# Hybrid attention block: the first branch's value products as [query, 64] from unnormalised probabilities

## The chip, the cores and the metric

The kernel runs on one core of a Trainium2 chip. The metric is the device time of one execution in microseconds (us). Before the change it is 987.19 us, the median of three runs (986.64 to 987.54).

## What is computed

One decoder layer on 512 tokens of width 1024 in float32: normalise, project, three attention branches, gate and merge, project, then a gated feed-forward part. The change touches the first branch alone. It has eight heads of width 64 and softmax over the keys that an index score has picked (the others are masked). The reference keeps a compressed latent of 128 numbers per token for all heads:

```python
# per block of 128 queries
logits = einsum('bqhc,bqkc->bqhk', ql, kv_sel) * ATTN_SCALE + bias
p = softmax(where(dist >= 0, logits, -inf))
o_lat = einsum('bqhk,bqkc->bqhc', p, kv_sel)
# outside
o_a = einsum('bshc,hce->bshe', o_lat, w_uv).reshape(B, S, -1)
merged = sigmoid(z_a) * (o_a @ w_branch_a) + ...
```

The kernel applies w_uv to the latent first, so that each head has values `va` of 64 columns per key, and the output of a head is the probabilities times `va`.

## The kernel before

Activations lie transposed (features on the 128 partitions, 512 tokens along the row) for the projections. A projection takes both operands as a high part (rounded to the matmul's own float32 form) and a low part (the rest), and makes three matmuls of them. "Split" below means that ScalarE copies the high part and VectorE subtracts it from the source.

Attention runs as one software pipeline of 88 steps, written out in the order in which each engine issues. Steps 0 to 31 are the third branch, 32 to 63 the first branch (head (v - 32) // 4, query block i = v % 4, over 128 (i + 1) keys), 64 to 79 the second branch, the rest drains. Up to step 63 two steps begin together, at even v. A step of the first branch goes through these stations:

- TensorE `scores` (L1175, L1176): two matmuls into one of the two banks of `s_ps`.
- VectorE `shift` (L2106): adds the bias and mask table, takes the row's extreme, writes `nl`. The table of a head comes from DRAM through SyncE's queue (L678, L680), into one of two buffers.
- ScalarE `exponentials` (L1646): the exponential, with the row sum in `expsum`.
- VectorE `reciprocal` (L2124), one column per step; GpSimd (L855) multiplies the probabilities by it.
- TensorE `transpose_probs` (L1194): 128x128 blocks through the identity into `t_ps`. ScalarE copies them to `pt` (L1658).
- TensorE `times_values` (L1226): per block of keys one matmul, weights `va` of two heads (128 columns), moving operand the transposed probabilities (128 queries). The result in `o_ps` is [values of two heads, queries], and 64 of its rows are used.
- After the four blocks of a head: ScalarE copies the high part of 64 rows to `oa_hi` (L1734), VectorE subtracts it to `oa_lo` (L2180).

The transposes of a pair of steps come at odd v, three for the narrower pair and seven for the wider, the products at even v. Beside the attention TensorE works on projections in `tile_ps`: value tiles bv 0 to 7 of the second branch (L1288 to L1290, four steps each, from step 34 on; each begun at an even step after the scores), key tiles (L1246) at steps 26, 35, 43, 49, the third branch's transposes `oc` (L1256) at 51 and 57, gate tiles z (L924 to L926) from step 66 on and transposes `ob` of the second branch (L1263). `attention_tiles` numbers these tiles in the order of the steps, and a tile uses bank number % 2 of `tile_ps`: it waits until the one before it in that bank has been emptied (`tile_start`). ScalarE empties bv and z tiles (L1508), one step after or at the end of the step in which they are finished, behind the exponentials of that step.

The buffers `o_ps` are two as well. A group of products waits for the output of the group before the last to have been read (`oa_read`).

Of the kernel before, what the change touches and what calls it, by code (L numbers as in the profile page):

```python
# [22 lines left out]
P = 128  # L23
# [127 lines left out]

def ob_at(v):

    return (v - 73) // 4 if 73 <= v <= 85 and (v - 73) % 4 == 0 else None
# [35 lines left out]
def attention_tiles():  # L190

    names = []
    for v in range(N_STEP):
        if dense_at(v) is not None and 0 in dense_at(v)[1]:
            names.append(dense_at(v)[0])
        names += latent_tiles_at(v)
        if v in OC_STEPS:
            names.append(("oc", OC_STEPS.index(v)))
# [33 lines left out]
def hybrid_block(nc, a, out):  # L232
# [10 lines left out]
    with ctx:  # L243
# [62 lines left out]
        w_ukt = place("w_ukt", R + 25, [P, S])  # L306
        va = place("va", R + 57, [P, NBLK, S])
# [173 lines left out]
        recip_made = sem("recip_made")  # L481
        normed = sem("normed")
# [291 lines left out]
        def _(pool):  # L774
# [76 lines left out]
            for v in range(MIX_A - 1, MIX_B + 16 + 1):  # L851
                if MIX_A <= v - 1 < MIX_B:
                    pool.wait_ge(recip_made, v - MIX_A)
                    b = nl_of(v - 1)[0][:, 0:width_of(v - 1)]
                    pool.tensor_scalar(b, b, recip[:, v - 1:v], 1.0, ALU.mult, ALU.mult).then_inc(normed, 1)  # L855
                if MIX_B <= v - 1 < N_MIX:
                    k = subs_of(v - 1)[1]
                    pool.wait_ge(recip_made, v - MIX_A)
# [41 lines left out]
        def _(pe):  # L900
# [282 lines left out]
            def transpose_probs(v):  # L1183
                if v < MIX_A:
                    pe.wait_ge(exped, v + 1)
                elif v < MIX_B:
                    pe.wait_ge(normed, v - MIX_A + 1)
                else:
                    pe.wait_ge(mixed, v - MIX_B + 1)
# [7 lines left out]
            def times_values(v):  # L1197
# [16 lines left out]
                for j in range(nj):  # L1214
# [9 lines left out]
                    elif v < MIX_B:  # L1224
                        i, t = v % 4, (v - MIX_A) // 8
                        mm = pe.matmul(o[:, i * P:(i + 1) * P], va[:, j, t * P:(t + 1) * P], p_j, **flags)  # L1226
# [8 lines left out]
            def latent_tile(kind, n):  # L1235
# [11 lines left out]
                else:  # L1247
                    mm = pe.matmul(tile_ps[b][:], kv_T[:, n * P:(n + 1) * P], w_uv[:].rearrange("p h e -> p (h e)"),
                                   start=True, stop=True)
                mm.then_inc(tile_made[b], 1)  # L1250
# [45 lines left out]
            for v in range(N_STEP):  # L1296
# [19 lines left out]
                for p in products_at(v):  # L1316
                    times_values(p)
                if v in OC_STEPS:
# [170 lines left out]
        def _(act):  # L1489
# [175 lines left out]
            for v in range(N_STEP):  # L1665
# [63 lines left out]
                for p in products_at(v):  # L1729
                    if MIX_A <= p < MIX_B and p % 4 == 3:  # L1730
                        g = p // 4
                        act.wait_ge(o_made[g % 2], g // 2 + 1)
                        h, d0 = (p - MIX_A) // 4, DH * ((p - MIX_A) // 4 % 2)
                        act.activation(oa_hi[d0:d0 + DH, h // 2, :], o_ps[g % 2][d0:d0 + DH, :], ACT.Copy) \  # L1734
                            .then_inc(att_hi, 1)
                    if MIX_B <= p and p % 4 == 3:
# [4 lines left out]
                        for i in range(NBLK):  # L1741
                            act.activation(junk_b[:, i * P:(i + 1) * P], o_ps[g % 2][:, i * P:(i + 1) * P], ACT.Square,
                                           scale=P ** -0.5, accum_out=ms_b[:, 4 * h + i:4 * h + i + 1]) \
                                .then_inc(ob_sq, 1)
                if ob_at(v) is not None:
# [140 lines left out]
        def _(dve):  # L1886
# [233 lines left out]
            def reciprocal(u):  # L2120
# [400 lines left out]
```

## Time and profile before

| | |
|---|---|
| median of 3 runs | 987.19 us |
| the profiled execution | 986.81 us |
| its span, first to last instruction | 985.0 us |
| granted TensorE clock, mean | 0.999 |
| busy: TensorE, VectorE, ScalarE, GpSimd | 969.2, 494.0, 379.9, 117.4 us |
| first branch, products on TensorE | 286.1 to 351.6 us |

The profile shows one execution. An instruction's row has its start and its duration in us, the engine, the line of the kernel, what it writes and reads, and in brackets how long the engine was idle before it and what released it. PE is TensorE, PEld its weight loads, DVE VectorE, ACT ScalarE, POOL GpSimd, SPq the DMA queue of SyncE. Matmuls overlap: the next starts well before the modelled end of the one before, so a pace is read from starts. A float32 matmul shows as two passes, a transpose as one.

### The profile page before, as it was taken

How to read it: one execution, taken by the hardware profiler on the slowest of the kernel's cores; microseconds unless marked ns; L12 is line 12 of the kernel's file. 1: busy time of each engine (PE TensorE's matmuls, PEld its weight loads, DVE VectorE, ACT ScalarE, POOL GpSimd, SP SyncE). 2: the span in 40 equal slices, each digit the busy share in tenths (PEclk: the TensorE clock that was granted, in tenths of full speed). 3: DMA queues.
4: the chain of work that ended last, by engine and by line, in shares of the span. 5: the costliest groups of instructions: out<-in, count | busy, mean ns of one | idle time of the engine just before them, and what ended most of it. 6: DMA issues, size and time to landing. Idle time of an engine off the chain costs nothing.

```text
span 985.0 us, 12729 instructions
## 1 busy us (share of the span) xinstructions
PE 969.2 (98%) x4913; PEld 802.9 (82%) x4913; DVE 494.0 (50%) x847; ACT 379.9 (39%) x685; POOL 117.4 (12%) x161
## 2 busy tenths in 40 slices
PE   7999999999999999999999999999999999999997
PEld 4778888878888977888788888988888888888886
DVE  4764778833457556465655555634334334321323
ACT  5355332255577766632222225432232222211322
POOL 1500000077023312100000011000000000000401
PEclk9999999999999999999999999999999999999999
DMA  8732845356335311264646651224443334232312
GB/s 329 241 123 86 275 131 167 111 169 221 97 89 170 114 33 44 74 226 139 214 138 214 246 171 43 78 73 124 146 148 114 106 106 149 86 110 83 129 43 86
DMA packets 91875, 134.13 MB, mean 136 GB/s; under 512 B 5464, under 2 KB 71605, under 8 KB 91698
## 3 DMA queue, kind: packets, MB, share of 16 engines
q1 hardware_dynamic: 89234, 120.18, 37.7%
q0 software_dynamic: 2448, 13.03, 4.1%
q8 instruction: 31, 0.51, 0.2%
q10 hardware_dynamic: 144, 0.26, 0.1%
q14 instruction: 18, 0.15, 0.0%
HBM read 125.01 MB, written 13.17 MB: 140 GB/s over the span
## 4 chain that ended last, share of the span: by engine, by line
PE 93%; issue 2%; POOL 2%; ACT 1%; DMA 1%; DVE 1%; SPq 0%; POOLq 0%; DVEq 0%
PE tile_ps L924 19%; PE tile_ps L925 18%; PE tile_ps L926 18%; PE t_ps L1194 2%; PE o_ps L1226 2%; PE tile_ps L1377 1%; PE s_ps L1377 1%; PE s_ps L1375 1%; PE t_ps L1377 1%; PE t_ps L1375 1%; PE tile_ps L1375 1%; PE tile_ps L1376 1%; PE s_ps L1376 1%; PE t_ps L1376 1%; PE s_ps L1179 1%
## 5 line engine op out<-in xcount | busy, mean ns | idle before, releaser
L924 PE MATMUL tile_ps<-h_hi,w_hi 128*128 128x512 f32 x736 | 291.1, 395 | 0.0
L925 PE MATMUL tile_ps<-h_lo,w_hi 128*128 128x512 f32 x736 | 286.9, 390 | 0.0
L926 PE MATMUL tile_ps<-h_hi,w_lo 128*128 128x512 f32 x736 | 286.7, 390 | 0.0
L1902 DVE TENSOR_TENSOR w_lo<-w_raw,w_hi 128x2048 fp32r<-128x2048 f32 (+3 forms) x60 | 130.7, 2179 | 155.2 <-ACT w_hi L1501 154.4
L924 PEld LDWEIGHTS tile_ps<-h_hi,w_hi 128*128 128x128 f32 x736 | 138.1, 188 | 36.1 <-issue 6.9
L926 PEld LDWEIGHTS tile_ps<-h_hi,w_lo 128*128 128x128 f32 x736 | 138.2, 188 | 29.4
L925 PEld LDWEIGHTS tile_ps<-h_lo,w_hi 128*128 128x128 f32 x736 | 138.3, 188 | 27.3 <-issue 0.2
L1501 ACT ACTIVATE w_hi<-w_raw 128x2048 fp32r<-128x2048 f32 (+3 forms) x60 | 107.3, 1788 | 40.8 <-DMA w_raw<-in_w_branch_c_dram 10.2
L1899 DVE TENSOR_TENSOR t_lo<-t_raw,t_hi 128x2048 fp32r<-128x2048 f32 (+1 forms) x15 | 32.7, 2183 | 85.6 <-ACT t_hi L1499 85.5
L1499 ACT ACTIVATE t_hi<-t_raw 128x2048 fp32r<-128x2048 f32 (+1 forms) x15 | 27.0, 1800 | 81.4 <-PE s_ps L1377 53.5
L1646 ACT ACTIVATE nl<-nl,cst 128x256 f32<-128x256 f32 (+3 forms) x81 | 42.6, 527 | 33.1 <-DVE cst L2106 33.0
L1849 ACT ACTIVATE f_hi<-f_t 128x512 f32 (+1 forms) x22 | 13.9, 633 | 88.3 <-DVE f_t L2428 88.3
L2428 DVE TENSOR_TENSOR f_t<-tile_ps,silu_t 128x512 f32<-128x512 f32 x20 | 13.8, 692 | 54.7 <-PE tile_ps L926 54.7
L1843 ACT ACTIVATE silu_t<-tile_ps 128x512 f32<-128x512 f32 x22 | 13.1, 598 | 72.0 <-PE tile_ps L926 71.9
L881 POOL TENSOR_TENSOR x<-gated,x 128x512 f32<-128x512 f32 x4 | 5.0, 1285 | 297.2 <-DVE gated L2349 297.2
L1658 ACT ACTIVATE pt<-t_ps 128x128 f32<-128x128 f32 (+2 forms) x80 | 29.2, 406 | 20.3 <-PE t_ps L1194 19.6
L855 POOL TENSOR_SCALAR nl<-nl,cst 128x128 f32<-128x128 f32 (+3 forms) x32 | 23.2, 731 | 76.6 <-DVE cst L2124 75.5
L2106 DVE CUSTOM_DVE_ANT_0 nl<-s_ps,tab 128x256 f32<-128x256 f32 (+3 forms) x49 | 22.2, 476 | 10.3 <-PE s_ps L1179 5.0
L2267 DVE SCALAR_TENSOR_TENSOR ada_sum<-ada,cst,ada_sum 128x1024 f32<-128x1024 f32 x21 | 26.9, 1283 | 0.7
L869 POOL TENSOR_TENSOR x<-gated,x_res 128x512 f32<-128x512 f32 x4 | 5.1, 1293 | 184.5 <-DVE gated L2349 184.5
L2056 DVE MAX8 cst<-score 128x8 f32<-128x256 f32 (+2 forms) x48 | 25.2, 552 | 1.4
L2064 DVE MATCH_REPLACE8 score<-cst,score 128x256 f32<-128x256 f32 (+2 forms) x48 | 25.8, 542 | 0.0
(413 smaller groups left out, 1709.0 us busy)
## 6 DMA issues: line engine op xcount, KB each, us to landing
w_raw<-in_w_in_dram SPq DMA_DIRECT2D x31, 1024.0 KB, 6.0
w_raw<-in_w_gate_up_dram SPq DMA_DIRECT2D x22, 1024.0 KB, 7.3
ada<-in_w_ada_dram SPq DMA_DIRECT2D x12, 1024.0 KB, 5.3
t_raw<-in_w_down_dram SPq DMA_DIRECT2D x10, 1024.0 KB, 5.1
row_copies<-row_flat POOLq DMA_DIRECT2D x1, 5632.0 KB, 21.4
ada<-in_w_ada_dram SPq DMA_DIRECT2D x8, 640.0 KB, 11.5
tab<-masked_tables SPq DMA_DIRECT2D x8, 576.0 KB, 5.6
ada<-in_w_ada_dram SPq DMA_DIRECT2D x8, 512.0 KB, 4.7
```

The source lines that it names most:

```text
L924: pe.matmul(dst[0:mw, :], wh, x_hi[:, kx, :], start=start, stop=False)
L925: pe.matmul(dst[0:mw, :], wh, x_lo[:, kx, :], start=False, stop=False)
L926: mm = pe.matmul(dst[0:mw, :], wl, x_hi[:, kx, :], start=False, stop=stop)
L1375: pe.matmul(bank[:], x_hi[:, kx, blk], wh[:, kw, :], start=start, stop=False)
L1376: pe.matmul(bank[:], x_hi[:, kx, blk], wl[:, kw, :], start=False, stop=False)
L1377: mm = pe.matmul(bank[:], x_lo[:, kx, blk], wh[:, kw, :], start=False, stop=stop)
L1499: act.activation(t_hi[s][:, 0:wide, :], t_raw[s][:, 0:wide, :], ACT.Copy).then_inc(w_hi_made[s], 1)
L1501: hi = nc.scalar.activation(w_hi[s][:, 0:kt, 0:n_cols], w_raw[s][:, 0:kt, 0:n_cols], ACT.Copy)
L1646: act.activation(b, b, ACT.Exp, bias=negmax[:, k:k + 1], scale=-1.0, accum_out=expsum[:, k:k + 1]).then_inc(exped, 1)
L1658: act.activation(pt[v % 2][:, 0:w], t_ps[v % 2][:, 0:w], ACT.Copy).then_inc(pt_ready, 1)
L1899: dve.tensor_tensor(t_lo[s][:, 0:wide, :], t_raw[s][:, 0:wide, :], t_hi[s][:, 0:wide, :].bitcast(F32), ALU.subtract).then_inc(w_split[s], 1)
L1902: dve.tensor_tensor(w_lo[s][:, 0:kt, 0:n_cols], w_raw[s][:, 0:kt, 0:n_cols], w_hi[s][:, 0:kt, 0:n_cols].bitcast(F32), ALU.subtract) \
```

## The change

The probabilities stay unnormalised. GpSimd's multiplication of them (L855) and its wait go, and the transposes wait for the exponentials instead. In `times_values` the operands change places: the transposed probabilities are the weights, 64 columns of `va` the moving operand, and `o_ps` holds [queries, 64] for each of the four blocks of a head. When a head is done, VectorE takes the reciprocal of its four row sums at once and multiplies the 256 columns by them while it copies them out of `o_ps` to a new buffer `oa_nat` (`norm_head`). When a pair of heads is done, at steps 45, 53, 61 and 69, TensorE transposes the pair's four 128x128 blocks into a new tile `oa` of `tile_ps` (`transpose_a`), and ScalarE and VectorE split it into `oa_hi` and `oa_lo`, 128x512 each. The four new tiles stand in `attention_tiles` and so move the numbers of those behind them.

```diff
+def oa_at(v):
+    return (v - 45) // 8 if 45 <= v <= 69 and (v - 45) % 8 == 0 else None
...
         names += latent_tiles_at(v)
+        if oa_at(v) is not None:
+            names.append(("oa", oa_at(v)))
...
-            for v in range(MIX_A - 1, MIX_B + 16 + 1):
-                if MIX_A <= v - 1 < MIX_B:
-                    pool.wait_ge(recip_made, v - MIX_A)
-                    b = nl_of(v - 1)[0][:, 0:width_of(v - 1)]
-                    pool.tensor_scalar(b, b, recip[:, v - 1:v], 1.0, ALU.mult, ALU.mult).then_inc(normed, 1)
+            for v in range(MIX_B, MIX_B + 16 + 1):
...
-                if v < MIX_A:
+                if v < MIX_B:
                     pe.wait_ge(exped, v + 1)
-                elif v < MIX_B:
-                    pe.wait_ge(normed, v - MIX_A + 1)
...
                     elif v < MIX_B:
-                        i, t = v % 4, (v - MIX_A) // 8
-                        mm = pe.matmul(o[:, i * P:(i + 1) * P], va[:, j, t * P:(t + 1) * P], p_j, **flags)
+                        i, h = v % 4, (v - MIX_A) // 4
+                        mm = pe.matmul(o[:, i * DH:(i + 1) * DH], p_j, va[:, j, h * DH:(h + 1) * DH], **flags)
...
+            def transpose_a(t):
+                b = tile_start(ATT_TILE["oa", t])
+                pe.wait_ge(oa_read, 2 * t + 2)
+                for r in range(NBLK):
+                    mm = pe.transpose(tile_ps[b][:, r * P:(r + 1) * P], oa_nat[:, t, r, :], ident[:])
+                mm.then_inc(tile_made[b], 1)
...
                 for p in products_at(v):
                     times_values(p)
+                if oa_at(v) is not None:
+                    transpose_a(oa_at(v))
...
-                    if MIX_A <= p < MIX_B and p % 4 == 3:
-                        g = p // 4
-                        act.wait_ge(o_made[g % 2], g // 2 + 1)
-                        h, d0 = (p - MIX_A) // 4, DH * ((p - MIX_A) // 4 % 2)
-                        act.activation(oa_hi[d0:d0 + DH, h // 2, :], o_ps[g % 2][d0:d0 + DH, :], ACT.Copy) \
-                            .then_inc(att_hi, 1)
...
+                if oa_at(v) is not None:
+                    split_hi(("oa", oa_at(v)), oa_hi[:, oa_at(v), :])
...
-            def reciprocal(u):
-
-                if MIX_A <= u < MIX_B:
-                    dve.wait_ge(exped, u + 1)
-                    dve.reciprocal(recip[:, u:u + 1], expsum[:, u:u + 1]).then_inc(recip_made, 1)
+            def norm_head(h):
+
+                c0 = MIX_A + 4 * h
+                dve.wait_ge(exped, c0 + 4)
+                link(dve.reciprocal(recip[:, c0:c0 + 4], expsum[:, c0:c0 + 4]))
+                dve.wait_ge(o_made[h % 2], (MIX_A // 4 + h) // 2 + 1)
+                dve.tensor_tensor(oa_nat[:, h // 2, :, DH * (h % 2):DH * (h % 2) + DH],
+                                  o_ps[h % 2][:, 0:CW].rearrange("p (i e) -> p i e", e=DH),
+                                  recip[:, c0:c0 + 4].unsqueeze(2).to_broadcast([P, NBLK, DH]), ALU.mult) \
+                    .then_inc(oa_read, 1)
...
-                    h = head_done_at(v - 1)
-                    d0 = DH * (h % 2)
-                    dve.wait_ge(att_hi, n_split + 1)
-                    dve.tensor_tensor(oa_lo[d0:d0 + DH, h // 2, :], o_ps[h % 2][d0:d0 + DH, :],
-                                      oa_hi[d0:d0 + DH, h // 2, :].bitcast(F32), ALU.subtract).then_inc(oa_read, 1)
-                    n_split += 1
+                    norm_head(head_done_at(v - 1))
...
+                if oa_at(v) is not None:
+                    split_lo(n_split, ("oa", oa_at(v)), oa_lo[:, oa_at(v), :], oa_hi[:, oa_at(v), :])
+                    n_split += 1
```

## Rows read from the trace of the kernel before

**Rows 1.** The page, part 1: busy time and share of the span, instructions.
```profile
PE 969.2 (98%) x4913; PEld 802.9 (82%) x4913; DVE 494.0 (50%) x847; ACT 379.9 (39%) x685; POOL 117.4 (12%) x161
```
**Rows 2.** The page, part 4: the chain that ended last, shares by engine.
```profile
PE 93%; issue 2%; POOL 2%; ACT 1%; DMA 1%; DVE 1%; SPq 0%; POOLq 0%; DVEq 0%
```
**Rows 3.** Waits of TensorE, 352 to 985 us: total, times, longest.
```profile
PE s_ps L1179 <- DVE cst L2106: 0.4, 2, 0.2
```
**Rows 4.** Waits of all engines, 286 to 352 us.
```profile
POOL nl L855 <- DVE cst L2124: 34.4, 14, 5.6
...
PE tile_ps L1288 <- ACT bv L1508: 1.1, 2, 0.7
...
PE s_ps L1175 <- DVE cst L2106: 0.5, 1, 0.5
...
PEld t_ps L1194 <- POOL nl L855: 0.3, 1, 0.3
```
**Rows 5.** Timeline of TensorE, 300 to 316 us: start, duration, instruction.
```profile
302.69 0.83 PE L1226 MATMUL o_ps<-pt,va 128*128 128x128 f32 x6
303.36 0.93 PE L1194 MATMUL t_ps<-ident,nl 128*128 128x128 f32 x7
...
305.22 0.40 PE L1175 MATMUL s_ps<-ak_st,aq_st 128*128 128x512 f32 x1
305.45 0.40 PE L1176 MATMUL s_ps<-al_st,aq_st 128*128 128x512 f32 x1
306.19 0.38 PE L1288 MATMUL tile_ps<-w_hi,h_hi 128*128 128x256 f32 x1 [0.34 <-ACT bv L1508]
...
315.52 0.36 PE L1288 MATMUL tile_ps<-w_hi,h_hi 128*128 128x256 f32 x1 [0.73 <-ACT bv L1508]
```
**Rows 6.** All instructions of L1226: duration ns, minimum, median, maximum.
```profile
L1226 PEld LDWEIGHTS o_ps<-pt,va x160: 188/192/192, 286.1 to 351.2; 128*128 128x128 f32 x160
L1226 PE MATMUL o_ps<-pt,va x160: 272/275/275, 286.2 to 351.3; 128*128 128x128 f32 x160
```
**Rows 7.** Timeline of the weight loads beside the first of rows 5.
```profile
302.57 0.76 PEld L1226 LDWEIGHTS o_ps<-pt,va 128*128 128x128 f32 x6
```
**Rows 8.** Timeline, 262 to 266 us: the third branch's products, [query, 64].
```profile
263.50 1.00 PE L1223 MATMUL o_ps<-cv,pt 128*128 128x64 f32 x8
263.50 0.86 PEld L1223 LDWEIGHTS o_ps<-cv,pt 128*128 128x128 f32 x7 [0.24 <-issue]
```
**Rows 9.** The chain that ended last, in order of time, 280 to 420 us.
```profile
330.48 0.44 PE tile_ps L1256 x4
```
**Rows 10.** Timeline of VectorE and ScalarE, 304 to 316 us.
```profile
304.41 0.29 DVE L2106 CUSTOM_DVE_ANT_0 nl<-s_ps,tab 128x128 f32<-128x128 f32 x1 [0.99 <-PE t_ps L1194]
...
305.76 0.38 ACT L1508 ACTIVATE bv<-tile_ps 128x256 f32<-128x256 f32 x1
...
313.00 0.28 DVE L2106 CUSTOM_DVE_ANT_0 nl<-s_ps,tab 128x128 f32<-128x128 f32 x1
...
314.99 0.39 ACT L1508 ACTIVATE bv<-tile_ps 128x256 f32<-128x256 f32 x1
```
**Rows 11.** Table of head 3: its issue (timeline); size, us to landing (DMA view).
```profile
295.73 0.45 SPq L680 DMA_DIRECT2D tab<-masked_tables  x1
...
tab<-masked_tables SPq DMA_DIRECT2D x1, 576.0 KB, 8.1
```
**Rows 12.** Timeline at step 53.
```profile
322.10 0.93 PE L1194 MATMUL t_ps<-ident,nl 128*128 128x128 f32 x7
...
323.09 0.39 ACT L1508 ACTIVATE bv<-tile_ps 128x256 f32<-128x256 f32 x1
```
**Rows 13.** Timeline at steps 71 and 72.
```profile
369.58 0.57 ACT L1508 ACTIVATE z<-tile_ps 128x512 f32<-128x512 f32 x1
369.77 0.50 PE L924 MATMUL tile_ps<-h_hi,w_hi 128*128 128x512 f32 x1
```
**Rows 14.** Groups by line, 286 to 352 us: busy us, mean ns of one, idle before.
```profile
L2180 DVE TENSOR_TENSOR oa_lo<-o_ps,oa_hi 64x512 fp32r<-64x512 f32 x7 | 4.8, 688 | 4.7 <-ACT oa_hi L1734 4.6
```

More of the change, by code:

```diff
@@ L306, in hybrid_block @@
         w_ukt = place("w_ukt", R + 25, [P, S])
+        oa_nat = place("oa_nat", R + 0, [P, 4, NBLK, P])
         va = place("va", R + 57, [P, NBLK, S])
@@ L849, in _ @@
                 masked_table(h)
-            for v in range(MIX_A - 1, MIX_B + 16 + 1):
-                if MIX_A <= v - 1 < MIX_B:
-                    pool.wait_ge(recip_made, v - MIX_A)
-                    b = nl_of(v - 1)[0][:, 0:width_of(v - 1)]
-                    pool.tensor_scalar(b, b, recip[:, v - 1:v], 1.0, ALU.mult, ALU.mult).then_inc(normed, 1)
+            for v in range(MIX_B, MIX_B + 16 + 1):
                 if MIX_B <= v - 1 < N_MIX:
                     k = subs_of(v - 1)[1]
-                    pool.wait_ge(recip_made, v - MIX_A)
+                    pool.wait_ge(recip_made, v - MIX_B)
                     b = nl_of(k)[0][:, 0:width_of(v - 1)]
@@ L2151, in _ @@
                     shift(subs_of(u)[0])
-                if v % 2:
-                    for u in (v - 1, v):
-                        reciprocal(u)
                 if v < MIX_B and lo_at(v) is not None:
@@ L2165, in _ @@
                     w = width_of(v - 1)
-                    dve.wait_ge(normed, v - MIX_A)
+                    dve.wait_ge(normed, v - MIX_B)
                     b0, b1 = nl_of(k0)[0][:, 0:w], nl_of(k1)[0][:, 0:w]
@@ L2252, in _ @@
                     n_split += 1
-            assert n_split == 2 + A_H + B_H
+            assert n_split == 2 + A_H // 2 + B_H
             def product(t, dst, gate):
```

## The prediction

> **What bounds the kernel now.** I read the page first. TensorE is busy for 969.2 of 985.0 us [rows 1] and the chain of work that ended last lies on it for 93% [rows 2]: whatever TensorE gains or loses inside the attention steps arrives at the end one for one, because what follows is TensorE's own work: from 352 us to the end it waits for another engine only 0.4 us in all [rows 3]. So the question is not what the engines around TensorE do, but two things: how many passes TensorE makes, and where it has to wait.
>
> Next the waits, for the stretch in which the eight heads of the first branch run (286 to 352 us) [rows 4]. Here the reader should see two sizes. GpSimd waits 34.4 us for VectorE's reciprocals, which says only that it has little to do. TensorE waits 1.1 us in two places for ScalarE to empty a value tile (bv), 0.5 us for VectorE, and 0.3 us for GpSimd's normalised probabilities. The last one is all that the scaling on GpSimd costs directly. The holes are somewhat larger than the idle time says, since a matmul's modelled end lies behind the point at which the next could start: two 512-column scores start at 305.22 and 305.45 and last 0.40 [rows 5], so the next was possible at 305.68 and came at 306.19, a hole of 0.5 where the row says 0.34. Counted so, the two holes at the value tiles are 0.5 and 0.9, the one behind VectorE 0.65 and the one behind GpSimd 0.2, 2.3 us in all.
>
> **Products.** 80 matmuls of 128 moving columns become 80 of 64. A float32 product runs as two passes, so 160 rows each. Six passes of the old kind take 0.83 us from the first start to the last end [rows 5]. One pass lasts 0.275 us and one weight load 0.192 [rows 6], so the starts are (0.83 - 0.275) / 5 = 0.111 us apart. So are the loads beside them: (0.76 - 0.19) / 5 = 0.114 [rows 7]. The third branch already has products in the new form, [query, 64] with the transposed probabilities as weights: eight passes take 1.00 us, (1.00 - 0.275) / 7 = 0.104, with their loads (0.86 - 0.19) / 6 = 0.112 apart [rows 8]. So the pace is that of the weight loads, whose number and size stay the same. I take the saving as 0. The most that these rows allow is (0.111 - 0.104) x 160 = 1.1 us, less because the shorter first pass in the old third branch follows a 512-column matmul and not a 256-column one. A loss has no row in its favour: the 64-column form is nowhere slower.
>
> The Trainium skill (TensorE: Matmul & The Clock Gate, "Back-to-back issue gap") gives an isolated matmul of 128 columns 134 cycles and one of up to 64 about 60. By this table alone 160 passes would save 160 x 74 cycles, some 4.9 us at the 2.4 GHz at which the rows stand. The same section says that in a stream both the load and the matmul set the pace, and with that the trace agrees: 0.111 us for either width.
>
> **Transposes added.** Four tiles of four 128x128 transposes. A transpose runs as one pass. Seven take 0.93 us [rows 5], some 0.11 from one to the next, and the chain shows the same thing done for the third branch, four transposes out of o_near, at 0.44 us [rows 9]. 4 x 0.44 = **1.76 us**, all of it on TensorE. Nothing covers it.
>
> **The banks of tile_ps.** This part is easy to miss. Tiles alternate between two banks in the order of attention_tiles, so each inserted tile turns over the parity of those behind it. I wrote out the order with the new tiles. Three places change whom TensorE waits for.
>
> Step 45: the new tile 0 takes the bank of bv tile 2, which ScalarE empties at 305.76 to 306.14 [rows 10], late, because the exponentials before it wait for VectorE, and VectorE starts them at 304.41 only when the masked table of head 3 is there: issued at 295.73, 8.1 us to landing, so 303.8 [rows 11]. (The row names TensorE as releaser, which had finished long before.) The change touches none of this. TensorE is through with its transposes at 304.1 and would stand until 306.2, then transpose (0.44), then make the scores of steps 46 and 47 (0.9) which before lay ahead of the wait: bv tile 3 starts at 307.5 instead of 306.19 [rows 5], 1.3 us later. But behind it stood another hole: bv tile 4 waits until 315.52 [rows 5] for bv tile 3 to be emptied at 314.99 [rows 10], 0.9 us. This one is set by VectorE, which works nearly without a break from the shift at 304.41 to the one at 313.00 [rows 10], for which ScalarE's exponentials wait and behind them the emptying. What the change does to VectorE there: one more subtraction of 512 columns (0.69, the price of the one that it now has per head [rows 14]), one such subtraction out, one multiply of 256 columns in (half the columns, so between 0.35 and 0.69), a reciprocal of four columns for four of one. That is 313.0 to 313.3 for the shift, and bv tile 3 is empty at 315.4 to 315.7. TensorE, 1.3 us late, gets there at 315.96 and doesn't wait. Net up to here: 0.44 us, the transposes themselves; the 0.2 us that GpSimd had cost is swallowed by the same table. Stall added: **0**, with ends at -0.4 (bv tile 4 starts at 315.52 after all) and +0.9 (the wait at 315 remains in full).
>
> Step 53: tile 1 takes the bank of bv tile 4. It is emptied at 323.09 + 0.39 = 323.5 [rows 12]. TensorE starts its seven transposes at 322.10 and is ready for the next thing 0.77 us later [rows 12], now 0.44 us after that, at 323.3: **0.17 us** of wait, between 0 and 0.65 (no shift of TensorE).
>
> Step 72: before, z tile 2 used another bank than z tile 1. With tile 3 in between (step 69) both have the same. z tile 1 is emptied from 369.58 to 370.15, z tile 2 starts at 369.77 [rows 13]; both hang on TensorE's scores and so move together. 370.15 + 0.05 - 369.77 = **0.43 us**, with 0 and 0.6 as ends. Tile 2 (step 61) and tile 3 (step 69) find their banks empty, one since step 57, the other since step 68.
>
> **What goes off the path at nothing.** 32 scalings on GpSimd: covered by the 34.4 us for which it stands idle anyway [rows 4]. Eight ScalarE copies of 64x512 against four of 128x512, and eight VectorE subtractions (0.69 each [rows 14]) against eight multiplies and four subtractions: VectorE's total hardly moves, cover is TensorE's own work except around 304 to 315, which is counted. VectorE's new wait is for the head's products: behind it stand the next shift and through it the next scores. Before it waited for the same products and for ScalarE's copy on top, so it leaves 0.6 us earlier. The wait for the new tiles' split at the end of steps 45, 53, 61, 69 holds up the next shift by some 0.7 to 1.4 us. At step 61 that is the worst, since VectorE was idle then; the probabilities of step 62 are still used only some 4 us later. No DMA is issued or moved.
>
> **The sum.** 1.76 + 0 + 0.17 + 0.43 = 2.36 us. On the profiled execution (span 985.0, its own time 986.81) that is 989.17. The median of the three runs shown, 987.19, lies 0.38 above it, and gives 989.55. Predicted: **989.5**. A measurement of this kernel can tell some 0.2% from no change, that is 2 us, and my sum lies just beyond.
>
> **Rivals.**
> (a) Not slower: the idle time of TensorE in this stretch is won back. Of the 2.3 us of holes [rows 4], the two at the value tiles and the one at the scores go away and don't return as the wait of tile 0, as VectorE, free of the wait for ScalarE's copy and of GpSimd beside it, reaches the shift of step 48 a microsecond early. Then 1.76 + 0.43 - 2.1 = +0.1: 987.3. It decides at one point: whether TensorE is held at step 45 beyond 305 us. The late table [rows 11] speaks against it; that VectorE has idle time before and after speaks for it. Chance 0.22, with the 1.1 us from the products' first passes counted as another way to get to 988.
> (b) More slower: the holes stay and the new waits come on top. At step 45 the 1.3 us aren't absorbed, since VectorE's extra subtraction also moves the emptying of bv tile 3, and step 53 and 72 cost their upper ends. 1.76 + 0.9 + 0.65 + 0.6 = 3.9: 991.1. For it: VectorE's queue at 304 to 313 is full. Chance 0.22.
> (c) Faster: the product passes go at the pace of their moving columns. The scores of 512 columns start at 305.22 and 305.45 [rows 5], 0.23 us apart or 0.45 ns a column; 64 columns less in 160 passes are 4.6 us. 989.55 - 4.6 = 985.0. The third branch's 64-column passes at 0.104 us speak against it. Chance 0.05. This is where the skill's table for an isolated matmul would lead.
> (d) The forecast, 988.9 to 990.2: chance 0.46. The remaining 0.05 is for what I don't see, on either side.
>
> **How the numbers follow.** Faster than 985.2: (c) and little else, 0.06. Within 0.2%, up to 989.16: (a) 0.22, and of the forecast's own range the lower third, 0.16, in all 0.38. Slower: 0.56. (a) reaches from 986.7 to 988.2 and (b) from 990.2 to 992. The range takes in most of both, 986.9 to 991.5; outside lie (c), the ends of (a) and (b) with some 0.1, and part of what I don't see, together a little under 2 in 10.
>
> **What the profile would show.** Products: six passes of 64 columns in 0.8 us, as before; if it is nearer 0.4, (c) holds. Four groups of four transposes at 0.44 us on the chain. A wait of TensorE of about 2 us at the first of them, on ScalarE's bv copy, and none at bv tile 4 any more; if both are there, (b), if neither, (a). A wait of 0.4 us before z tile 2 on ScalarE's z copy. GpSimd without its 32 scalings, with no effect on the span. What would make the prediction wrong above all is my hand-made order of VectorE's work between 304 and 315 us, where 0.3 us here or there decides whether one wait replaces another or adds to it.

## The result

The changed kernel takes 988.71 us (median, 987.81 to 990.08) where the kernel before, run beside it, takes 987.31. The ratio is 1.0015, with a 95% interval of 1.0008 to 1.0022: slower by 0.8 to 2.2 us. The median lies inside the 0.2% that I had named as the bound of "same", and the interval reaches just beyond it.

The profiled execution took 989.13 us, against 986.81 before. The page of the changed kernel, span, part 1 and the chain's shares of part 4, to be held against [rows 1, 2]:

```profile
span 987.3 us, 12716 instructions
...
PE 971.1 (98%) x4929; PEld 805.5 (82%) x4929; DVE 490.9 (50%) x827; ACT 378.5 (38%) x681; POOL 94.9 (10%) x129
...
PE 93%; issue 2%; POOL 1%; ACT 1%; DVE 1%; DMA 1%; SPq 0%; POOLq 0%; DVEq 0%
```

TensorE has 16 instructions and 1.9 us more, GpSimd 22 us less, and the chain lies on TensorE as before. That the profiled execution came out at the 989.17 us of my sum is a coincidence. Laid instruction against instruction, the two traces are 1.22 us apart before the first branch begins, in code that is the same in both. Among all the profiles of this case the first transpose of probabilities starts anywhere from 205.6 to 207.9 us. What the change does has to be read from there on. I use one measure for all kernels, the **stretch**: from the first transpose of probabilities to the last transpose of the second branch's output (`olat`), start to start. Everything behind it takes 575.4 to 575.7 us in every trace. For the changed kernel, all instructions of these two lines (duration ns: minimum, median, maximum; first start and last end):

```profile
L1197 PE MATMUL t_ps<-ident,nl x160: 270/273/329, 206.9 to 398.0; 128*128 128x128 f32 x160
...
L1273 PE MATMUL tile_ps<-ident,olat x16: 272/273/273, 378.9 to 411.7; 128*128 128x128 f32 x16
```

The same two of the kernel before:

```profile
L1194 PE MATMUL t_ps<-ident,nl x160: 270/273/329, 205.6 to 395.9; 128*128 128x128 f32 x160
...
L1263 PE MATMUL tile_ps<-ident,olat x16: 270/272/273, 376.7 to 409.6; 128*128 128x128 f32 x16
```

With two decimals the stretch is 203.92 us before and 204.81 after: **+0.9 us**, not the 2.36 of my sum. The waits of all engines between 286 and 353 us in the changed kernel answer to [rows 4], and those of TensorE from 353 us to the end to [rows 3]:

```profile
POOL nlb L865 <- DVE cst L2170: 104.8, 1, 104.8
...
DVE cst L2209 <- DMA o_far<-far_rows: 3.9, 1, 3.9
...
PEld tile_ps L1259 <- ACT bv L1520: 1.9, 2, 1.8
...
PE tile_ps L1259 <- ACT bv L1520: 1.5, 1, 1.5
```
```profile
PE tile_ps L929 <- ACT z L1520: 0.5, 1, 0.5
PE s_ps L1184 <- DVE cst L2114: 0.4, 2, 0.2
```

Both waits that I had named are there. The first new tile (L1259) waits for ScalarE's emptying of a bv tile, and z tile 2 (L929) for that of z tile 1; the wait at bv tile 4 [rows 5] has gone. The timeline of TensorE at the first new tile:

```profile
303.77 0.78 PE L1229 MATMUL o_ps<-va,pt 128*128 128x64 f32 x6
304.39 0.94 PE L1197 MATMUL t_ps<-ident,nl 128*128 128x128 f32 x7
306.85 0.65 PE L1259 MATMUL tile_ps<-ident,oa_nat 128*128 128x128 f32 x4 [1.53 <-ACT bv L1520]
307.26 0.42 PE L1180 MATMUL s_ps<-ak_st,aq_st 128*128 128x384 f32 x1
```

Counted from starts this hole is 1.69 us. The holes of the kernel before, 2.3 us in all, have become this one and one of 0.27 at 293 us, 2.0 in all, not counting what the new tiles add at steps 53 and 72 (below). And the six product passes take 0.78 us where they took 0.83 [rows 5]. That small number is the part that I had dismissed.

### The profile page after: what moved, and what is told of

It is laid out like the page before. It is cut to its first block, busy times and chain, and to the rows that moved or that the text cites. A ratio compares the mean times of both kernels' runs of the same rounds, so it can differ in the third digit from the quotient of the medians.

```text
span 987.3 us, 12716 instructions
## 1 busy us (share of the span) xinstructions
PE 971.1 (98%) x4929; PEld 805.5 (82%) x4929; DVE 490.9 (50%) x827; ACT 378.5 (38%) x681; POOL 94.9 (10%) x129
## 4 chain that ended last, share of the span: by engine, by line
PE 93%; issue 2%; POOL 1%; ACT 1%; DVE 1%; DMA 1%; SPq 0%; POOLq 0%; DVEq 0%
PE tile_ps L929 19%; PE tile_ps L931 18%; PE tile_ps L930 18%; PE t_ps L1197 2%; PE o_ps L1229 2%; PE tile_ps L1388 1%; PE tile_ps L1387 1%; PE s_ps L1388 1%; PE s_ps L1387 1%; PE t_ps L1388 1%; PE t_ps L1387 1%; PE tile_ps L1389 1%; PE s_ps L1389 1%; PE t_ps L1389 1%; PE o_ps L1387 1%
## 5 line engine op out<-in xcount | busy, mean ns | idle before, releaser
L929 PE MATMUL tile_ps<-h_hi,w_hi 128*128 128x512 f32 x736 | 291.0, 395 | 0.5 <-ACT z L1520 0.5
L929 PEld LDWEIGHTS tile_ps<-h_hi,w_hi 128*128 128x128 f32 x736 | 138.1, 188 | 36.2 <-issue 7.5
L1197 PE MATMUL t_ps<-ident,nl 128*128 128x128 f32 x160 | 24.5, 275 | 0.0
L1197 PEld LDWEIGHTS t_ps<-ident,nl 128*128 128x128 f32 x160 | 19.2, 149 | 5.8 <-issue 3.8
```

What stands on the lines that cost most here:

```text
L929: pe.matmul(dst[0:mw, :], wh, x_hi[:, kx, :], start=start, stop=False)
L1197: mm = pe.transpose(t_ps[v % 2][:, j * P:(j + 1) * P], src[:, j * P:(j + 1) * P], ident[:])
```

## The experiments

Each ran beside the kernel before on the same chip. The stretches, with all of the later kernels:

| kernel | stretch, us | median, us | before beside it | ratio, 95% interval |
|---|---|---|---|---|
| before | 203.92 | 987.31 | | |
| c_before | 203.61 | 988.65, one run | 987.48 | |
| after | 204.81 | 988.71 | 987.31 | 1.0015, 1.0008 to 1.0022 |
| c_after | 205.12 | 988.42 | 987.61 | 1.0009, 1.0000 to 1.0018 |
| wide128 | 205.03 | 989.27 | 987.48 | 1.0017, 1.0009 to 1.0026 |
| twice | 206.62 | 990.74 | 987.48 | 1.0031, 1.0020 to 1.0043 |
| no_scaling | 203.73 | 987.18 | 987.48 | 0.9993, 0.9985 to 1.0002 |
| oa3_late | 204.21 | 988.04 | 987.61 | 1.0009, 1.0000 to 1.0018 |
| table_first | 204.91 | 987.93 | 987.61 | 1.0000, 0.9991 to 1.0009 |
| both | 204.75 | 987.97 | 987.61 | 1.0001, 0.9992 to 1.0011 |
| far_early | 203.05 | 987.02 | 987.69 | 0.9991, 0.9982 to 1.0000 |
| all_three | 202.93 | 986.98 | 987.69 | 0.9993, 0.9984 to 1.0002 |
| before_far_table | 201.73 | 985.97 | 987.69 | 0.9982, 0.9973 to 0.9991 |
| before_far | 201.81 | 985.66 | 987.35 | 0.9983, 0.9974 to 0.9992 |

**c_before and c_after: the same code again.**

> The kernel before, unchanged, for a second trace. In the first pair of traces the changed kernel is already 1.2 us behind at the start of the attention steps (first transposes of probabilities at 206.9 against 205.6 us), where no instruction differs. If that is scatter of the start-up, the first transposes here stand anywhere between 205 and 207.5 us and the stretch from them to the last transposes of the second branch is again 204.0 us within 0.1. If it were a property of the code, both numbers repeat: 205.6 and 409.6.

> The changed kernel, unchanged, on the same chip as the variants, for their difference to it. It should be 1.0 to 1.5 us over before, with the stretch from the first transposes of probabilities to the last of outputs at 204.8 us.

These are the two kernels unchanged. The stretch repeats to 0.31 us for either one (203.92 and 203.61; 204.81 and 205.12). The whole time doesn't repeat so well: c_before's stretch is the shorter one, and yet its run is 1.8 us longer than the profiled one of before (988.65 against 986.81), because it began the stretch at 207.8 instead of 205.6. From these two pairs I take it that a stretch tells some 0.5 us apart and one whole run some 2 us, and the price of the change from two traces each is 0.9 to 1.5 us.

The 0.31 us of c_after have a place. The far rows (see table_first) land later in it, the exponentials behind VectorE come later, and the six product passes ahead of the hole at step 45 are drawn out by 0.33 us; the hole is as long as in after. The row of these passes, to be held against the 0.78 above:

```profile
302.78 0.93 PE L1229 MATMUL o_ps<-va,pt 128*128 128x64 f32 x6
```

**wide128: the products with 128 moving columns again.** The weights stay the transposed probabilities, the moving operand is `va` of both heads of the pair, and half of the result isn't used. `norm_head`, not shown here, picks the head's 64 columns out of each 128.

```diff
-                        mm = pe.matmul(o[:, i * DH:(i + 1) * DH], p_j, va[:, j, h * DH:(h + 1) * DH], **flags)
+                        mm = pe.matmul(o[:, i * P:(i + 1) * P], p_j, va[:, j, h // 2 * P:(h // 2 + 1) * P], **flags)
```

> The changed kernel with one size put back: the moving operand of the value products is the 128 columns of a head pair instead of the head's 64, the rest stays. Theory 1 (the first pass of each group of products is shorter with 64 columns, 0.060 against 0.113 us, and 16 groups save 0.85 us): the first passes are 0.113 us again, the stretch from the first to the last transposes of probabilities and outputs (204.8 us in the changed kernel) grows to 205.6, in the timed runs 0.8 us over the changed kernel, some 2.2 us over before. Rival (the 0.8 us that the sum missed came from less waiting, not from the width): the stretch stays 204.8.

The stretch alone settles nothing: 205.03 lies between the two of the changed kernel, since the hole at step 45 happened to be 1.41 us here. The passes do. Groups of 14 product passes behind this hole, first in the changed kernel, then here:

```profile
309.60 1.67 PE L1229 MATMUL o_ps<-va,pt 128*128 128x64 f32 x14
```
```profile
310.41 1.73 PE L1229 MATMUL o_ps<-va,pt 128*128 128x128 f32 x14
```

The trace's single passes show where the 0.06 comes from. Within a group all passes but the first are 0.112 us from start to start at either width. Only the first is different: 0.113 us with 128 moving columns, 0.060 with 64. There are 17 groups of product passes, and over all of them the first passes sum to 1.91 us in before and in wide128, and to 1.01 in the changed kernel. From the first start of a group to the instruction behind it, the 17 groups take 18.13 us against 17.23. So the narrower operand shortens the passes by **0.90 us**.

Not all of it reaches the end. The stretch grew by 0.22 us and the hole shrank by 0.28, so 0.50 arrives in this pair, where I had expected 0.8. Between 307 and 352 us wide128 falls behind the changed kernel from 0.82 to 1.26 us, 0.44 for twelve groups at 0.053: the key tile behind one of them starts its second pass after 0.431 us instead of 0.485, and the hole at step 53 is 0.05 shorter. The timed runs can't show it: the ratio is 1.0017, with 1.0015 and 1.0009 for the changed kernel. The row of the weight load beside it shows how a group of 64 columns is passed (changed kernel):

```profile
303.65 0.76 PEld L1229 LDWEIGHTS o_ps<-va,pt 128*128 128x128 f32 x6
```

The loads are as far apart as before [rows 7] and pace both forms. In a run of passes of 64 columns, the next load starts 0.053 us after a matmul's start; with 128 columns it starts 0.002 after it. The loads thus stand half a pass further ahead, and the rows show it won once per group.

**twice: each new tile is transposed two times.**

```diff
-                for r in range(NBLK):
+                for r in (*range(NBLK), *range(NBLK)):
```

> The changed kernel with each of its 16 new transposes made twice. Theory 1 (the transposes lie on the path in full, 0.11 us each): 0.44 us per tile, 1.76 us over the changed kernel, the stretch from the first to the last transposes 206.5 us. Rival (a part of them hides in waits that are there anyway): the first tile, behind which the wait for ScalarE and VectorE stands, costs nothing or little more, and the whole is 1.3 us or less.

All instructions of the line, and the last ones of the stretch:

```profile
L1259 PE MATMUL tile_ps<-ident,oa_nat x32: 272/273/332, 306.3 to 364.7; 128*128 128x128 f32 x32
...
L1273 PE MATMUL tile_ps<-ident,olat x16: 270/273/275, 380.1 to 412.8; 128*128 128x128 f32 x16
```

Another 16 transposes make the stretch 1.5 us longer than c_after's and 1.8 longer than after's. Laid against c_after instruction by instruction, each of the four tiles takes 0.44 us more, 1.75 in all; the rest is the drawn-out product passes of c_after. Nothing hides them. At these four places transposes stand on the path in full.

**no_scaling: GpSimd's scaling alone taken out of the kernel before.**

```diff
-                    pool.tensor_scalar(b, b, recip[:, v - 1:v], 1.0, ALU.mult, ALU.mult).then_inc(normed, 1)
```

> The kernel before without GpSimd's multiplication of the first branch's probabilities; transposes wait for the exponentials. Left out: the normalisation of the first branch. Theory 1 (GpSimd's scaling costs 0.2 us at step 39 and this is swallowed by the late table of head 3): the hole at step 39 goes, TensorE's wait before the scores of step 46 grows by as much, the time is that of before within 0.2 us. Rival (normalised probabilities hold the pipeline up in more places, or GpSimd slows VectorE): 0.5 to 1.5 us faster, with smaller holes between 304 and 316 us.

The transposes wait for the exponentials, as in the changed kernel, and the first branch stays unnormalised. 203.73 us lies between the two stretches of before (203.92 and 203.61), the ratio's interval contains 1, and the holes at 304 to 315 us are 0.81, 0.51 and 0.55 against 0.65, 0.51 and 0.90. The hole of 0.2 us inside the transposes at 292 us is gone, and the next scores come 0.28 us later instead. GpSimd's 22 us were worth nothing that can be measured here, 0.2 us at most.

**oa3_late: the fourth new tile six steps later.** At step 75 instead of 69 it lies behind the z tiles, so that z tiles 1 and 2 are in different banks again.

```diff
-    return (v - 45) // 8 if 45 <= v <= 69 and (v - 45) % 8 == 0 else None
+    return {45: 0, 53: 1, 61: 2, 75: 3}.get(v)
```

> The changed kernel with its fourth output tile at step 75 instead of 69. Then z tile 1 and z tile 2 use different banks again. Theory 1 (the fourth tile's place in the order of the banks costs 0.43 us, as the next gate tile must wait for the emptying of the one before): TensorE's wait of 0.5 us on ScalarE's z copy is gone, the stretch is 204.4 us, the time 0.4 us under the changed kernel. Rival (something else holds TensorE there, or the wait moves on to the next gate tile): the stretch stays 204.8.

In the changed kernel z tile 2 waits for ScalarE's emptying of z tile 1, as worked out from [rows 13]:

```profile
371.21 0.57 ACT L1520 ACTIVATE z<-tile_ps 128x512 f32<-128x512 f32 x1
...
371.93 0.47 PE L929 MATMUL tile_ps<-h_hi,w_hi 128*128 128x512 f32 x1 [0.47 <-ACT z L1520]
```

With the tile at step 75 that wait is gone, 0.51 us, and so are the 0.44 us of the tile's transposes: at step 75 they fit into a hole between scores. But most of both comes back. The first of it is at step 77, 0.29 us: VectorE's scaling of `olat` now stands behind the moved split and has moved forward by less than TensorE, and TensorE's transposes of it start late (oa3_late, first the operand's writer, then the transposes):

```profile
390.82 0.34 DVE L2247 TENSOR_SCALAR olat<-o_ps,cst 128x128 f32<-128x128 f32 x1
...
391.31 0.63 PE L1273 MATMUL tile_ps<-ident,olat 128*128 128x128 f32 x4
```

The stretch is 204.21. Against after it is 0.60 shorter, of which 0.44 is the smaller hole at step 45 (1.25 instead of 1.69). That leaves 0.16 of the 0.95 that was taken out; the rest comes back after the transposes of `olat`, at the scores (0.2) and at the second branch's products behind them (0.2), where TensorE waits 0.19 us for ScalarE's copy of the probabilities. So the expected 204.4 was met thanks to the smaller hole. The z wait is real, but a place that isn't crowded is harder to find than I had thought. all_three against far_early says the same, 0.12.

**table_first and both: the late table of head 3.** I had put the hole at step 45 down to this table [rows 11]. Here it is issued ahead of a weight load of 1 MB instead of behind it; `both` has the fourth tile at step 75 on top.

```diff
-                if n == 2:
+                if n == 3:
                     load(21, [(KT, 0, cols(COL_Z + D, CW))])
```

> The changed kernel with two loads exchanged in SyncE's queue: the mask table of head 3 goes ahead of the 1 MB weight chunk that stands before it. Theory 1 (the hole of 1.7 us at the first output tile comes from that table's landing at 303.8 us): it lands some 3 us earlier, VectorE starts on head 3 without waiting, about 1.3 us earlier, and the hole is 0.4 us; the stretch is 203.5 to 203.9 us, the time 0.9 to 1.3 us under the changed kernel. Rival (VectorE's own work between 300 and 313 us sets it): the hole stays over 1.2 us or comes back at the value tile behind it, and less than 0.4 us is gained.

> The two together: the fourth output tile at step 75 and the table ahead of the weights. If the two causes are independent, the gains add: stretch 203.1 to 203.5 us, time 1.3 to 1.7 us under the changed kernel, so level with the kernel before or just under it.

The transfers of table_first as SyncE issues them:

```profile
294.74 0.37 SPq L697 DMA_DIRECT2D o_far<-far_rows  x1
295.54 0.32 SPq L687 DMA_DIRECT2D tab<-row_copies  x1
295.91 0.42 SPq L689 DMA_DIRECT2D tab<-masked_tables  x1
296.38 0.43 SPq L613 DMA_DIRECT2D w_raw<-in_w_in_dram  x1
```

The table lands 3 us earlier, 14.4 us after the first product instead of 17.4. **The hole doesn't move**: 1.69 us, stretch 204.91. `both` has 204.75, where gains that add would have given 203.1 to 203.5. What the waits between 286 and 320 us of table_first show instead:

```profile
DVE cst L2209 <- DMA o_far<-far_rows: 5.5, 1, 5.5
...
PE tile_ps L1259 <- ACT bv L1520: 1.5, 1, 1.5
```

VectorE stands for 5.5 us at another transfer. At the end of the third branch a part of its output (`o_far`) goes out to DRAM and is read back in another order, and VectorE meets this reading back at step 41, ahead of the shift that needs the table of head 3. That shift in the changed kernel, then in table_first:

```profile
305.07 0.29 DVE L2114 CUSTOM_DVE_ANT_0 nl<-s_ps,tab 128x128 f32<-128x128 f32 x1 [1.46 <-PE t_ps L1197]
```
```profile
305.09 0.29 DVE L2114 CUSTOM_DVE_ANT_0 nl<-s_ps,tab 128x128 f32<-128x128 f32 x1
```

In the changed kernel VectorE was held 3.9 us by the far rows and 1.46 us by the table; here it was held 5.5 us by the far rows and not at all by the table, and started the shift at the same time. So either transfer can set the hole, and freeing one leaves the other. The same wait stands in the trace of before, shorter, beside the rows of [rows 4]:

```profile
DVE cst L2204 <- DMA o_far<-far_rows: 1.8, 1, 1.8
```

The exchange didn't make the far rows late: c_after and twice, where the table stands in its old place, have waits of 5.7 and 5.4 us for them too. When they land (11.2 to 12.9 us after the first product) varies between executions of one kernel, and the hole at step 45 follows the start of this shift, counted from the first product: 1.25 us at 17.1 (oa3_late), 1.41 at 17.4 (wide128), 1.69 at 17.6 and 17.7 (after, table_first). That the exchange is worth nothing holds for this execution. Where the far rows land as early as in after, it may be worth something: the timed runs of table_first are 0.5 us under those of c_after on the same chip, with intervals that meet (1.0000, up to 1.0009, against 1.0009, down to 1.0000), and this isn't settled. Both transfers stand behind the store of the far rows in SyncE's queue, and the next kernels move that.

**far_early: only the store of the far rows moved.** SyncE issued it behind a copy of the keys and the table of head 2. Now it goes ahead of both; the reading back stays where it was.

```diff
-                if n == 2:
+                if n == 1:
                     sp.wait_ge(far_packed, 1)
                     sp.dma_start(far_dram.rearrange("(p r) n -> p r n", r=4), o_far[:]).then_inc(far_stored, 16)
+                if n == 2:
                     sp.wait_ge(far_stored, 16)
```

**all_three** has the edits of oa3_late and table_first besides. **before_far** has this edit alone, in the kernel before, and **before_far_table** that one and the table's.

> The changed kernel with one transfer issued earlier in SyncE's queue: the store of the third branch's far outputs (528 KB to DRAM, to be read back in another order) goes ahead of the key copies and of the table of head 2. Theory 1, new after the exchange of table and weights had moved the table 3 us ahead and the hole not at all: the hole at the first output tile (1.7 us) hangs on a chain of transfers that bind VectorE one after the other, first the reading back of the far rows (wait of 3.9 us at step 41), then the table. With the store 3 to 4 us earlier both land before VectorE wants them; its wait at step 41 is gone, the hole is 0.8 us or less, the stretch from first to last transposes 203.6 to 204.1 us against 204.8, the time 0.7 to 1.2 us under the changed kernel. Rival (VectorE's own work sets it): the wait at step 41 is gone, the hole stays over 1.2 us.

> The changed kernel with all three moves: far store early, table of head 3 ahead of the weight chunk, fourth output tile at step 75. Theory 1: no transfer is late, the hole at the first output tile is under 0.4 us, no wait for the z copy; the stretch is 202.7 to 203.3 us, 1.5 to 2 us under the changed kernel and 0.6 to 1 us under the kernel before. Rival (the value tile's wait at step 50 comes back in full, 0.9 us): 203.6 to 204.0 us.

> The kernel before with the same two moves in SyncE's queue (far store early, table ahead of the weights). Theory 1 (its three holes between 304 and 316 us, 2.1 us in all, hang on the same transfers): at least 1.2 us of them go, the stretch is 202.3 to 202.7 us against 203.6 to 203.9. The change then costs about what its transposes cost less the shorter first passes, 0.5 to 0.9 us. Rival (they are of VectorE's and ScalarE's own making): the stretch stays over 203.3 us.

> The kernel before with the far store issued early and nothing else, the partner of far_early, which is the changed kernel with the same move (stretch 203.05 us, no late transfer left). Theory: without the holes that the transfers make, the change costs TensorE what its parts say: four tiles of transposes 1.76, less 17 shorter first passes 0.90, less the hole behind GpSimd 0.2, plus the z tile's wait 0.43, in all 1.1 us; so the stretch here is 201.7 to 202.1 us. Rival (the exchange of table and weights did the work in before_far_table, 201.73): the stretch here is over 202.8 us, with TensorE waiting at steps 46 to 50.

SyncE's queue, first in the changed kernel, then in far_early:

```profile
289.14 0.43 SPq L695 DMA_DIRECT2D far_rows<-o_far  x1
294.72 0.37 SPq L697 DMA_DIRECT2D o_far<-far_rows  x1
```
```profile
284.39 0.32 SPq L694 DMA_DIRECT2D far_rows<-o_far  x1
286.09 1.11 SPq L672 DMA_DIRECT2D ak_st<-ak_st  x2
...
288.37 0.44 SPq L697 DMA_DIRECT2D o_far<-far_rows  x1
```

SyncE waited for the store (5.6 us from issue to landing, among other transfers) before it could issue the reading back, the weights and the table. Issued earlier, ahead of the key copies and the table, the store takes 2.6 us, and everything behind it in the queue moves forward: the far rows land 7.1 us after the first product instead of 11.2, the table 11.9 instead of 17.4. VectorE no longer waits at step 41, and TensorE goes through step 45 (far_early):

```profile
303.01 0.78 PE L1229 MATMUL o_ps<-va,pt 128*128 128x64 f32 x6
303.63 0.94 PE L1197 MATMUL t_ps<-ident,nl 128*128 128x128 f32 x7
304.40 0.60 PE L1259 MATMUL tile_ps<-ident,oa_nat 128*128 128x128 f32 x4
304.75 0.42 PE L1180 MATMUL s_ps<-ak_st,aq_st 128*128 128x384 f32 x1
```

The stretch falls from 204.81 to 203.05, by the hole that was there (1.69, and 0.06 at the first transpose behind it), and further than the 203.6 to 204.1 that I had expected. The kernel before gains more from the same edit, since it had 2.3 us of holes: 2.1 of them go, and the stretch is 201.81. What is left are 0.2 us at GpSimd's probabilities, 0.24 at bv tile 4 and 0.17 at the transposes `oc` of step 51:

```profile
L1194 PE MATMUL t_ps<-ident,nl x160: 270/273/329, 206.2 to 394.4; 128*128 128x128 f32 x160
...
L1263 PE MATMUL tile_ps<-ident,olat x16: 270/272/273, 375.2 to 408.0; 128*128 128x128 f32 x16
```

With the table's exchange on top it is 201.73, no difference, and 0.6 us under what I had expected. So the store's place in the queue is the cause of most of the holes of before as well, and with it moved the table needs no help. before_far and before_far_table are the fastest versions, not to be told apart: 985.66 us (984.96 to 986.32) and 985.97, ratios 0.9983 (0.9974 to 0.9992) and 0.9982, without the change studied here. And with the disturbance gone from both sides, the change costs 203.05 - 201.81 = **1.24 us**.

## Why the prediction was right or wrong

I laid the traces against each other instruction by instruction, from start to start, over the whole stretch. That gives each term of the sum its measured size, in us:

| | forecast | before to after | before_far to far_early |
|---|---|---|---|
| four new tiles of transposes | 1.76 | 1.75 | 1.75 |
| first passes of the 17 product groups | 0 | -0.90 | -0.90 |
| given back at key tiles and one bv tile | | 0.13 | 0.13 |
| hole at GpSimd's probabilities, 292 us | 0 | -0.08 | -0.07 |
| holes from step 45 to bv tile 4 | 0 | -0.57 | -0.24 |
| hole at step 51 | | -0.19 | -0.17 |
| hole at step 53 | 0.17 | 0.16 | 0.16 |
| z tile 2, step 72 | 0.43 | 0.51 | 0.51 |
| all else, 0.03 or less each | | 0.08 | 0.09 |
| sum (rounded) | 2.36 | 0.89 | 1.24 |

**Transposes added: right.** 1.75 us, on the path in full, and twice has the same for 16 more.

**Products: the failed step is "I take the saving as 0".** It was 0.90 us in the passes, of which 0.13 were given back behind them. That the weight loads set the pace was right (0.112 us either way), and rival (c) is refuted: six passes took 0.78 us and not 0.4. But I saw the difference of the third branch's passes [rows 8], divided it evenly among the passes as 0.104 against 0.111, and put it down to the matmul in front. It wasn't a pace. In the trace the first of those eight starts 0.055 us ahead of the second and the others 0.112. Eight passes with a first one of 0.06 and six others of 0.112 give (0.06 + 6 x 0.112) / 7 = 0.105, which is the row's 0.104. The upper end that I kept, 1.1 us, had nearly the right size, though it was worked out from a pace that isn't there. And the sentence that TensorE's gains inside the attention steps arrive at the end one for one was too strong for the first branch: wide128 shows 0.50 of the 0.90 arriving.

**Step 45: the wait was forecast, but "Stall added: 0" was 0.57 us too high, and the cause only half right.** The wait at the new tile replaces the two holes at the value tiles and the one before the scores, as forecast, and bv tile 4 has no wait. But it is 1.69 us instead of about 2.1, and 1.75 with the longer first transpose, where the three holes of before make 2.32 counted in the same way. The difference lies below the lower end of -0.4. The shift of step 44 starts 17.6 us after the first product, and in before 18.2, though the table lands at 17.4 and 17.6: in before, c_before and no_scaling that shift starts 0.6 us after the table's landing, in after and wide128 0.2. Why, the traces don't show.

The cause that I named, the late table of head 3, is the last to land ahead of that shift in this trace, but not what has to be mended: with the table 3 us earlier nothing changed, as the far rows held VectorE as long. What both hang on is the store of the far rows, which far_early shows by taking the hole away. I missed it because the wait for those rows stands at VectorE one pair of shifts before the hole, 1.8 us long in the trace of before. The sentence "no DMA is issued or moved" was true, and the holes that the change inherits were still made by DMAs. Where no transfer is late, the mechanism of rival (a) shows: the shift of step 44 starts 14.9 us after the first product in far_early and 15.9 in before_far, and the hole at bv tile 4 goes.

**Step 53: right, 0.16 us against 0.17, in part by luck.** The changed kernel, to be held against [rows 12]:

```profile
322.68 0.94 PE L1197 MATMUL t_ps<-ident,nl 128*128 128x128 f32 x7
...
323.11 0.39 ACT L1520 ACTIVATE bv<-tile_ps 128x256 f32<-128x256 f32 x1
...
323.55 0.66 PE L1259 MATMUL tile_ps<-ident,oa_nat 128*128 128x128 f32 x4
```

Against the trace of before TensorE's seven transposes start 0.58 us later, where I had put 0.44, and ScalarE's emptying 0.02 us later. It ends at 323.50, TensorE is ready 0.77 us after 322.68, at 323.45, and starts at 323.55. That is 0.1 us, and another 0.05 because the first of the four transposes takes 0.16 us instead of 0.11. TensorE came later than I had put it, and the start behind the emptying cost what I had left out.

**Step 51, not in the forecast.** In before TensorE stood 0.19 us ahead of and in the transposes `oc`, where the profile shows a weight load waiting 0.2 us for VectorE's split of a key tile (L2144); in the changed kernel it doesn't.

**Step 72: right, 0.51 us against 0.43.** It is the one part of the sum that comes from nothing but the order in which tiles are numbered.

**GpSimd: right.** Its hole of 0.2 us at 292 us went and came back at the next scores, all but 0.08; no_scaling confirms it.

**The sum.** The 2.36 us of the forecast were 1.1 too high where no DMA disturbs, and 1.5 and 0.9 too high in the two pairs of kernels as they are, mainly by the products (0.90) and the holes behind step 45 (0.57). The medians say 1.4. Slower was right as a direction, and the median lies on the "same" side of the bound. The time, 989.5, came out 0.8 us above the measured 988.71. It lies inside the range because that was wide enough to take in rival (a) too, not because the sum was right.

**What stays open.** Why the first 206 us differ by up to 2.3 us from one execution to the next isn't explained. The first place where the traces of before and after drift apart for good is at 17 us, where one group of small projections takes some 0.1 us more a pass over ten passes; no kernel here touches it. The hardware's reason for the first pass of 0.060 us wasn't tested beyond the two widths 64 and 128. And why the far rows take 3.9 us to be read back in one execution of the changed kernel and 5.4 in another isn't known.

## What to carry to other kernels

Multiply a per-instruction price only by the instructions that show it: look at the first of a group apart from its successors before an average is called a pace. Adding a tile to a rotation of two banks changes who waits for whom far behind it, and writing out the order by hand found the two new waits and missed the one that went. And a wait on a table or a weight in DRAM is only the last one of its queue: look at what the queue itself was waiting for, here a store of half a megabyte, issued 4 us earlier, was worth 1.8 us of the stretch, where the whole restructuring costs 0.9 to 1.5.

## What the runs showed of the hardware

- With 64 moving columns instead of 128 and the same float32 weights of 128x128, only the first pass of a group is faster, 0.060 against 0.113 us; all others start 0.112 us apart, the pace of their weight loads. The Trainium skill (TensorE: Matmul & The Clock Gate, "Back-to-back issue gap") has some 134 and 60 cycles for isolated matmuls of the two widths; at the 2.4 GHz of these rows (granted clock 1.00) that would be, as an estimate, 0.056 and 0.025 us. The difference of 74 cycles for 160 passes would be 4.9 us by that estimate; measured were 0.90.
- A store of 528 KB landed after 2.6 to 2.7 us where it was issued ahead of the key copies and the table (far_early, all_three, before_far, before_far_table), and after 5.5 to 6.1 us behind them. Reading it back took 3.9 to 5.6 us, and differed as much between two executions of one kernel (3.9 in after, 5.4 in c_after).
- The store's place in the queue changed no bytes. The waits that it caused stood at VectorE (far rows, table), and through VectorE and ScalarE at TensorE, in the kernel before up to some 20 us after its landing (293.9 and 315.5 us).
